# Moving the addresses of matmul operands: distances of 224 and 0 bytes between moving columns and the next weights

## What is computed

```python
# first_block, for each layer l
h = rms_norm(x, pre_norm_g[l]);  proj = h @ w_in[l]            # 1024 -> 3328
y = concatenate([ya, yb], axis=-1) @ w_out[l]                 # 1024 -> 1024
x = x + rms_norm(y, post_norm_g[l])
# second_block, for each layer l
h = h + even_mixer(hn, ...)  if l % 2 == 0 else  h + odd_mixer(hn, ...)
#   even: p = h @ w_in (1024 -> 5192), ... @ w_out (1536 -> 1024)
#   odd:  h @ w_in (1024 -> 3072), ... @ w_out (1024 -> 1024)
h = h + conv_ffn(rmsnorm(h, norm_ffn[l]), ...)
# conv_ffn(h): u = h @ w_up; g = conv(h @ w_gate) + conv_b; (silu(g) * u) @ w_down   (1024 -> 2816 -> 1024)
```

## Time and profile before

| | |
|---|---|
| median of three runs | 2301.12 us |
| the profiled execution | 2309.54 us, its span 2307.8 us |
| TensorE busy (matmul) | 2217.0 us, 96% of the span, 14840 matmul records |
| VectorE busy | 1129.9 us, 49% |
| ScalarE busy | 966.7 us, 42% |
| GpSimd busy | 620.7 us, 27% |
| bytes moved by DMA | 175.64 MB, 76 GB/s over the span |

### The profile page before, as it was taken

One profiled execution on the slowest core, in us unless ns is written; L12 is line 12 of the kernel. 1 busy time (PEld: TensorE's weight loads), 2 busy tenths in 40 slices (PEclk: granted clock), 3 DMA queues, 4 the chain that ended last, 5 costly groups with the idle time before them and its releaser, 6 DMA issues. The chain is left out here.

```text
span 2307.8 us, 35487 instructions
## 1 busy us (share of the span) xinstructions
PE 2217.0 (96%) x14840; PEld 1974.6 (86%) x14840; DVE 1129.9 (49%) x1684; ACT 966.7 (42%) x1404; POOL 620.7 (27%) x480
## 2 busy tenths in 40 slices
PE   8999999998999999998999999999999989999998
PEld 6887579886589987886899999998988879988987
DVE  3458635557452234796444434444555534433443
ACT  4346634356543335435433313334655533322332
POOL 2112320123214325337123302322333212320321
PEclk8999999999999989999999999999999999999999
DMA  6341023310122212130233233222111013324322
GB/s 191 125 149 50 0 74 102 94 53 6 38 78 92 74 47 62 55 121 4 68 96 91 77 107 95 80 86 82 38 56 56 19 56 92 92 78 114 92 82 74
DMA packets 235315, 175.64 MB, mean 76 GB/s; under 512 B 7704, under 2 KB 230160, under 8 KB 234644
## 3 DMA queue, kind: packets, MB, share of 16 engines
q1 hardware_dynamic: 234836, 173.20, 25.2%
q10 hardware_dynamic: 320, 0.17, 0.0%
HBM read 171.20 MB, written 10.09 MB: 79 GB/s over the span
## 5 line engine op out<-in xcount | busy, mean ns | idle before, releaser
L347 DVE TENSOR_TENSOR panel_lo<-panel_raw,panel_hi 128x2048 fp32r<-128x2048 f32 (+2 forms) x148 | 332.0, 2243 | 252.7 <-ACT panel_hi L340 252.6
L340 ACT ACTIVATE panel_hi<-panel_raw 128x2048 fp32r<-128x2048 f32 (+2 forms) x150 | 266.8, 1778 | 368.2 <-PE product L450 252.6
L450 PE MATMUL product<-scaled_hi,panel_hi 128*128 128x256 f32 (+2 forms) x1232 | 282.4, 299 | 2.6 <-PEq L506 1.4
L450 PE MATMUL product<-scaled_hi,panel_lo 128*128 128x256 f32 (+2 forms) x1232 | 282.5, 299 | 0.0
L450 PE MATMUL product<-scaled_lo,panel_hi 128*128 128x256 f32 (+2 forms) x1232 | 282.2, 299 | 0.0
L450 PEld LDWEIGHTS product<-scaled_hi,panel_hi 128*128 128x128 f32 x1232 | 200.7, 188 | 11.5 <-issue 2.9
L450 PEld LDWEIGHTS product<-scaled_hi,panel_lo 128*128 128x128 f32 x1232 | 198.4, 188 | 7.4
L450 PEld LDWEIGHTS product<-scaled_lo,panel_hi 128*128 128x128 f32 x1232 | 198.2, 189 | 6.7
L463 PE MATMUL product_banks<-panel_hi,scaled_hi 128*128 128x256 f32 x696 | 194.7, 280 | 0.0
L463 PE MATMUL product_banks<-panel_hi,scaled_lo 128*128 128x256 f32 x696 | 194.4, 279 | 0.0
L463 PE MATMUL product_banks<-panel_lo,scaled_hi 128*128 128x256 f32 x696 | 194.4, 279 | 0.0
(11 more groups left out here) (599 smaller groups left out, 5440.9 us busy)
## 6 DMA issues: line engine op xcount, KB each, us to landing
panel_raw<-in_w_in_dram SPq DMA_DIRECT2D x26, 1024.0 KB, 5.4
panel_raw<-in_ffn_w_gate_dram SPq DMA_DIRECT2D x44, 512.0 KB, 4.0
panel_raw<-in_ffn_w_up_dram SPq DMA_DIRECT2D x44, 512.0 KB, 5.3
panel_raw<-in_ffn_w_down_dram SPq DMA_DIRECT2D x32, 704.0 KB, 4.7
panel_raw<-in_even_w_in_dram SPq DMA_DIRECT2D x21, 1024.0 KB, 5.3
panel_raw<-in_odd_w_in_dram SPq DMA_DIRECT2D x12, 1024.0 KB, 5.2
panel_raw<-in_w_out_dram SPq DMA_DIRECT2D x8, 1024.0 KB, 6.2
panel_raw<-in_even_w_out_dram SPq DMA_DIRECT2D x8, 768.0 KB, 5.3
```

Source lines behind the costliest of these rows:

```text
L340: act.activation(panel_view(c.hi[g % 2], product), raw_view(c.raw[g % 2], product), ACT.Copy).then_inc(c.hi_made.sem, 1)
L347: dve.tensor_tensor(panel_view(c.lo[g % 2], product), raw_view(c.raw[g % 2], product), panel_view(c.hi[g % 2], product).bitcast(F32), ALU. ...
L450: done = pe.matmul(banks[b], weight(w, k), a[:, k, u:v], start=(k == 0 and x == 0), stop=(k == chunks - 1 and x == 2))
```

## The change

It moves addresses and changes one order. Nothing is added to or taken from what is computed.

- A segment of a product gets `at`, the place (in elements of 4 bytes) at which its `panel_hi` and `panel_lo` begin in their buffers. First layers: 56 (phase 224) for wide tiles of `into`, 0 for row tiles. Even layer: 48 (phase 192) for the pairs of `selected`, 0 otherwise. Odd layer: 16 (phase 64) for the value tiles, 0 otherwise. All others are at 0.
- `SCALED_PHASES` are now pairs, for the high and the low part: 224 in the first layers and the even one, 32 in the odd layer and the first FFN, 224 and 32 in the second FFN. `y` of the even layer, `q` and the first FFN's `inner` go to 32.
- In the panels of the second FFN the up columns stand 32 bytes behind the gate columns (`gap=GAP`), so that the copies that make the panels go by halves (`halves_of`).
- In `wide_tile`, the opening tile of the even output and the odd layer's H tiles the order is hi-hi, lo-hi, hi-lo by panel and activation, where it was hi-hi, hi-lo, lo-hi. In the odd layer's row tiles it is now lo-hi, hi-hi, hi-lo. `row_tile` keeps its order.
- `eps` becomes a column of an 8-column tile `small`, in which one `rstd` finds room too.

```diff
-SCALED_PHASES = {0: 64, 1: 64, 4: 64, 5: 64, 6: 192, 7: 192}
+GAP = STEP // 2
+SCALED_PHASES = {0: (224, 224), 1: (224, 224), 4: (224, 224), 5: (32, 32), 6: (32, 32), 7: (224, 32)}
 Y_PHASES = (0, 0)
-EVEN_Y_PHASE, QUERY_PHASE = 192, 192
-INNER_PHASES = (192, 0)
+EVEN_Y_PHASES, QUERY_PHASES = (32, 32), (32, 32)
+INNER_PHASES = ((32, 32), (0, 0))
+ROWS_AT, WALK_AT = (0, 0), (0, 0)
+FLAT_AT, OUT_AT, WIDE_AT, PAIR_AT, VALUES_AT = (0, 0), (0, 0), (56, 56), (48, 48), (16, 16)
...
-    def __init__(self, panels, load, tiles, take):
-        self.panels, self.load, self.tiles, self.take = panels, load, tiles, take
+    def __init__(self, panels, load, tiles, take, at=(0, 0)):
+        self.panels, self.load, self.tiles, self.take, self.at = panels, load, tiles, take, at
...
-def panel_view(slot_tile, product):
-    rows = slot_tile[:, 0:product.chunks * product.pitch].rearrange("p (k n) -> p k n", k=product.chunks)
-    return rows[:, :, 0:product.cols]
+def halves_of(rows, product):
+    if not product.gap:
+        return rows
+    half = product.cols // 2
+    return rows.rearrange("p k (j n) -> p k j n", j=2) if rows.shape[2] == product.cols else bass.AP(
+        rows.tensor, rows.offset, [*rows.ap[:2], [half + product.gap, 2], [1, half]])
+
+
+def panel_view(slot_tile, product, at=0):
+    first = max(at + product.cols - product.pitch, 0)
+    rows = slot_tile[:, first:first + product.chunks * product.pitch].rearrange("p (k n) -> p k n", k=product.chunks)
+    return rows[:, :, at - first:at - first + product.cols + product.gap]
...
-        for x, (w, a) in enumerate(((w_hi, act_hi), (w_hi, act_lo), (w_lo, act_hi))):
+        for x, (w, a) in enumerate(((w_hi, act_hi), (w_lo, act_hi), (w_hi, act_lo))):
...
-            segments.append(Segment(1, columns(w_in, 1024 * third + 256 * group, 256), tiles, None))
+            segments.append(Segment(1, columns(w_in, 1024 * third + 256 * group, 256), tiles, None, VALUES_AT if third == 2 else WALK_AT))
...
-                        for x, (w, a) in enumerate(((w_hi, parts.hi), (w_hi, parts.lo), (w_lo, parts.hi))):
+                        order = ((w_lo, parts.hi), (w_hi, parts.hi)) if tile.kind == "N" else ((w_hi, parts.hi), (w_lo, parts.hi))
+                        for x, (w, a) in enumerate((*order, (w_hi, parts.lo))):
...
-        products.append(Product(c, KD, 256, [Segment(FF_HALF, load_inner, T_tiles(), None)], dmas=2, step=STEP))
+        products.append(Product(c, KD, 256, [Segment(FF_HALF, load_inner, T_tiles(), None, (0, 0) if layer else WALK_AT)], dmas=2, step=STEP, gap=GAP if layer else 0))
...
-                            wide_tile(pe, out, lambda w, k, j=j: w[:, k, P * j:P * (j + 1)], w_hi, w_lo, parts.hi, parts.lo, KD, tokens,
+                            at = (P + products[0].gap) * j
+                            wide_tile(pe, out, lambda w, k, at=at: w[:, k, at:at + P], w_hi, w_lo, parts.hi, parts.lo, KD, tokens,
```

More of the change, by code:

```diff
@@ L171, in open_core @@
     c.ones = sb("ones", [P, P])
-    c.eps = sb("eps", [P, 1])
+    c.small = sb("small", [P, 8])
+    c.eps = c.small[:, 0:1]
     c.gains = sb("gains", [P, N_GAINS, KD])
@@ L320, in extend, with views @@
         return first
+    def views(self, g):
+        c, (product, seg, _, _) = self.c, self.list[g]
+        return tuple(panel_view(t[g % 2], product, at) for t, at in zip((c.hi, c.lo), seg.at))
     def load(self, sp, g):
@@ L782, in chunk @@
                     tile, g = tile_at(at)
-                    w_hi, w_lo = (panel_view(t[g % 2], product) for t in (c.hi, c.lo))
+                    w_hi, w_lo = panels.views(g)
                     for x, (w, a) in enumerate(((w_hi, parts.hi), (w_hi, parts.lo), (w_lo, parts.hi))):
@@ L3188, in even_layer @@
             with ExitStack() as stage:
-                parts = [c.sb(f"y_{n}", [P, 12, TOK], F32R, into=stage, phase=EVEN_Y_PHASE) for n in ("hi", "lo")]
+                parts = [c.sb(f"y_{n}", [P, 12, TOK], F32R, into=stage, phase=phase) for n, phase in zip(("hi", "lo"), EVEN_Y_PHASES)]
                 ahead = ahead_of_ffn(c, ahead_stage, 0)
@@ L3713, in odd_layer @@
     with ExitStack() as layer:
-        q = [c.sb(f"q_{part}", [P, KD, TOK], F32R, into=layer, phase=QUERY_PHASE) for part in ("hi", "lo")]
+        q = [c.sb(f"q_{part}", [P, KD, TOK], F32R, into=layer, phase=phase) for part, phase in zip(("hi", "lo"), QUERY_PHASES)]
         odd_stage(c, into, q, taken, ahead)
@@ L3766, in __init__ @@
         self.total = c.sb("square_total", [P, self.tiles * P if whole else tokens], into=stage)[:] if total is None else total
-        self.rstd = c.sb("rstd", [P, NB2], side=side, into=stage if held is None else held)
+        self.rstd = c.sb("rstd", [P, NB2], side=side, into=stage if held is None else held)[:] if rstd is None else rstd
         self.pending = 0
@@ L3861, in __init__ @@
         self.c, self.src, self.gain, self.tokens, self.pending = c, src, gain, tokens, 0
-        self.hi, self.lo = (c.sb(f"scaled_{n}", [P, KD, room or tokens], F32R, side, into=stage, phase=SCALED_PHASES.get(gain))
-                            for n in ("hi", "lo"))
+        self.hi, self.lo = (c.sb(f"scaled_{n}", [P, KD, room or tokens], F32R, side, into=stage, phase=phase)
+                            for n, phase in zip(("hi", "lo"), SCALED_PHASES[gain]))
     def act_hi(self, act, k):
@@ L3978, in ffn_layer @@
             ahead.behind(1)
-        hi, lo = (c.sb(f"inner_{n}", [P, FF_HALF, width], F32R, into=stage, phase=INNER_PHASES[layer])
-                  for n in ("hi", "lo"))
+        hi, lo = (c.sb(f"inner_{n}", [P, FF_HALF, width], F32R, into=stage, phase=phase)
+                  for n, phase in zip(("hi", "lo"), INNER_PHASES[layer]))
         gated = [c.sb(f"gate{j}", [P, width + 2], into=stage) for j in range(2)]
@@ L4165, in two_blocks @@
             taken = c.sb("q_taken", [P, TOK], into=layer)
-            ahead = Ahead(c, layer, 5, None, taken[:], own.norm.squares, True)
+            ahead = Ahead(c, layer, 5, None, taken[:], own.norm.squares, True, c.small[:, 1:1 + NB2])
             ffn_layer(c, 0, ffn[0], own, ahead)
```

63 lines of the change are left out of this document (32 added, 31 removed).

## The result

| | before | after |
|---|---|---|
| median of 20 runs | 2302.23 us | 2310.81 us |
| ratio after / before | | 1.003, 95% interval 1.002 to 1.0039 |
| the profiled execution | 2309.54 us, span 2307.8 | 2313.38 us, span 2311.6 |
| mean granted clock in it | 0.982 | 0.978 |

The change makes the kernel slower by 0.3%. The forecast was 2279.5 us, 21.6 us faster; the time lies above its range as well.

A forecast was written before the change was run, and what follows sets the result against it. TensorE, busy in 96% of the span, was taken to bound the kernel through matmul spacing. Gains of 5.2 + 8.7 + 7.7 = 21.6 us came off the median 2301.1 us, giving 2279.5 us, range 2260 to 2305.

The forecast's parts named there:

- The bound: Whole kernel: TensorE is never fed too late, so time is the number of matmuls by the spacing between starts.
- The floor: Fastest spacing, 0.44 ns a column: 113 ns at 256 columns, 226 at 512; estimated 120 at 272, 107 at 242.
- Step 1: 512-column tiles of the first layers and second FFN's up tiles, moved to distance 0: 5.2 us gained, taken whole.
- Step 2: Row tiles, distance 64 to 224: two thirds of 13.1 us of room, 8.7 us gained.
- Step 3: Pairs of 256 and 272 columns, to 224 within a chunk: one third of 23.0 us of room, 7.7 us gained.
- Step 4: Second FFN's gate pairs (242 and 272 columns): 5.8 us of room, nothing booked.
- The rest: New order of forms and the gap's split panel copies: nothing; shifted attention tiles: 3 us either way, left to the range.
- D: Rival: slower, 224 acts like 192 and 128, row tiles at 283 ns; 2310 us; decided past 281 ns; chance 0.16.
- C: Rival: nothing measurable, the rhythm is set by where a stage's first stall falls, not by distance; 2301 us; chance 0.14.

The follow-up runs named there:

- the bursts: Separate kernels running only TensorE matmuls with this kernel's addresses at chosen distances, nothing of the reference computed; row tiles 113.3 to 123.6 ns by distance.
- before_again: The kernel before, unchanged, run and profiled a second time: median 2303.71 us, ratio 0.9997.
- order_only: The kernel after with all addresses of before and no gap, so only the new order of forms remains: one run, 2305.71 us.
- after_again: The kernel after, unchanged, run and profiled a second time: median 2310.47 us, ratio 1.0025 to before.
- walk64: The kernel after with only the walking tiles of the first FFN, odd layer and even output put back to old phases: 2306.72 us, ratio 0.9999 to before.
- uneven_rows: The kernel after with most tiles at old distances, high and low parts on separate phases in first FFN, even output and even-layer row tiles: 2300.43 us, 0.9983 to before.

## Why the prediction was wrong

**The bound: right.** All 7.5 us of added excess are in the spacing between matmuls; no wait took its place.

**The floor: right for one shape by itself.** No burst goes under 113.3 and 226.7 ns, 0.44 ns a column. For pairs it stayed an estimate: none came nearer than 238.3 to its 233.7.

**Step 1, half right.** The first layers' 512s went to 225 ns; the excess fell by 1.5 to 2.4 us where 2.9 were booked. The second FFN's up tiles, 2.3 us booked, gave nothing (394 ns as before, excess 2.43 to 2.60). The step that failed was to take the down product's 389 as what distance 0 gives: there the phases stay from chunk to chunk, in the up tiles they walk. In the bursts, walking 512s at distance 0 within a chunk and 64 at its end have 231.5 ns, not 226.7; and the changed kernel, whose up tiles have 0 at the chunk's end too, shows that taking the 64 away gains nothing.

**Step 2, wrong, and the largest error.** 8.7 us were booked as gained; the row tiles' excess rose. Two things failed. The room (13.1 us) came from one execution that had drawn the slow rhythm in the even layer. It was 10.5 us there (8.3 in the first and even layers and 2.1 in the odd one), but 4.2 and 5.4 in the other profiles of before. The prediction took the sum off a median 8.4 us under the profiled execution, "with the same work"; by those two profiles the executions around the median mostly had less room than the profiled one. And distance 224 was given two thirds of it because "a distance nearer 0 should leave the slow rhythm". 224 does leave the slow rhythm, and the fast one with it: 116.7 ns always, between 113.3 and 117.8. At 0 itself a row tile has 120.0. The check written down for this step, 276 in all stretches, failed in the first profile of after (279). Against before_again it costs 7.5 us, against the profiled before 1.1.

**Step 3, wrong in sign.** Room 23.0 against 22.4 measured, so the room was right. 7.7 us booked as gained; the even layer's pairs gave 0.5, the first FFN lost 1.7 and the odd layer about 0.8. The nearest rows were used as if the pace changed evenly with distance, and for all pairs alike. It doesn't: for walking pairs 224 is 1 ns worse than 64, in the kernel (242.8 against 241.7 ns) as in the bursts, and every uniform distance is worse than the best uneven mix (238.3). Only where the phases stay did 224 pay: the even layer's selected pairs went from 243.2 to 240.2 ns, as the bursts that stay have it (243.2 at 192, 239.9 at 224).

**Step 4.** Nothing booked, 0.5 us gained.

**The rest.** Order and gap at nothing: order_only agrees for the order by its excess. For the gap alone no run was made; TensorE's waits are no longer in after.

**The rivals.** D was right in sign and, by accident, near in size: its mechanism (row tiles at 283 ns) did not come about, and its point of decision, 281, was not reached either. The loss has another form, the fast rhythm being lost. C's thought, that what runs before a stage settles its rhythm, fits distance 64 and not 224, at which no run showed a second one. The Trainium skill's rule of two independent read ports ("TensorE: Matmul & The Clock Gate", "Step-by-step: what each phase is for") would make all distances equal; the bursts have 113.3 to 123.6 ns for the same row tile, and the measurement decides.

**What was chance.** From profile to profile the excess is almost equal, 44.2 and 44.6 us. The spans differ by 3.8 us. The clock was 0.982 and 0.978, or 83 and 102 us at the lower level, which is 0.31 x 19 = 5.8 us by the fit, more than the whole difference; the rest lies within the fit's 2 us. after_again has 0.982, so the lower clock of that one execution isn't put down to the change.

**Open.** Why the distance matters at all, and why each tile has its own curve, no run here shows. The bursts went in steps of 32 bytes from 0 to 224; that addresses 256 bytes apart are alike was not tested by itself. Nor is it known how often an execution draws the fast rhythm: seven profiles are few. The timed runs give a hint: levelled times scatter more where the even layer is at 64 (standard deviations of 2.1 to 3.9 us, 3.1 over all of them) than in after, after_again, walk64 and uneven_rows (1.1 to 2.2 us, 1.9 over all), as they would if 5 us were drawn in the first group and not in the second.

## What to carry to other kernels

A gain is taken off the median, so the room must be that of a typical execution: where one shape shows two paces in one profile, profile the same kernel again before booking the slower one as room. A dependence that has no model isn't to be interpolated; a kernel of bursts with the exact shape, order and walk of the addresses gives the whole curve in one run, and its differences of 1 ns came back in the kernel (walking pairs 241.7 and 242.8 ns, row tiles 116.7). Where the bursts didn't have the exact case (uneven distances in pairs that stay), the guess missed by 2.5 ns. And where one of two rhythms is the fastest pace of all, a value that only avoids the slow one (224) loses the fast one too.

## What the runs showed of the hardware

- At fp32r with 128 x 128 weights, the address distance from the moving columns to the next weights, modulo 256 bytes, moves a 256-column matmul from 113.3 to 123.6 ns, a pair of 256 and 272 columns from 238.3 to 248.6 (walking), and a 512-column one from 226.7 to 234.2 (one burst, or two or three, for each case).
- The same instructions at the same addresses can run in either of two steady paces (276 and 281 ns of printed duration) for a whole stage, by what ran before and by chance; in the slow one the weight load takes 192 ns, not 188.
- The best distance differs by kind of tile: 0 is the best for 512 columns whose phases stay and among the worst for row tiles. It differs too by whether the addresses walk: 239.9 ns a pair at 224 where they stay, 242.7 where they walk.
- Each us at the lower clock level costs this kernel 0.31 us in the fit over its profiles, and profiles of one kernel differ by up to 19 us in time at that level, about 6 us of span.
